# Small projection as 392 columns of one product, and a local values product on half the columns

## The reference

```python
qa, ka, va, ga, qi, ki, wi, qb, kb, vb, gb = jnp.split(proj, offsets, axis=-1)
# group A, blocks of 128 queries: an indexer scores the keys, the best 256 are kept
dots = jnp.einsum('bqhd,bsd->bqhs', qi_blk, ki)                   # 4 heads of 64
score = jnp.einsum('bqh,bqhs->bqs', w_blk * idx_scale, jax.nn.relu(dots))
_, idx = lax.top_k(jnp.where(visible[None], score, -jnp.inf), 256)
...                                                   # softmax attention over these, 8 heads
# group B: attention in a window of 128, 8 query heads on 2 key heads, a sink per head
out = jnp.einsum('bckgqs,bcskd->bcqkgd', p, v_band)
...
y = jnp.concatenate([ya * silu(ga), yb * silu(gb)], axis=-1) @ w_out
x = layer_norm(ALPHA * x + y, ln_g, ln_b)
```

## Time and profile before

| | |
|---|---|
| median of 3 runs | 1456.59 us (1453.73 to 1456.72) |
| the profiled execution | 1462.23 us, of which its span is 1460.4 us |
| TensorE (PE) busy | 1359.3 us, 93% |
| VectorE (DVE) busy | 1130.6 us, 77% |
| ScalarE (ACT) busy | 896.8 us, 61% |
| GpSimd (POOL) busy | 629.6 us, 43% |
| mean granted TensorE clock | 0.964 |

### The profile page before, as it was taken

One profiled execution on the slowest core, in us unless ns is written; L12 is line 12 of the kernel. 1 busy time (PEld: TensorE's weight loads), 2 busy tenths in 40 slices (PEclk: granted clock), 3 DMA queues, 4 the chain that ended last, 5 costly groups with the idle time before them and its releaser, 6 DMA issues. The chain is left out here.

```text
span 1460.4 us, 18810 instructions
## 1 busy us (share of the span) xinstructions
PE 1359.3 (93%) x6006; PEld 993.5 (68%) x6052; DVE 1130.6 (77%) x2215; ACT 896.8 (61%) x1687; POOL 629.6 (43%) x726
## 2 busy tenths in 40 slices
PE   7999999899999995798999799999999799999997
PEld 5888887698888874565655456655555565588886
DVE  3486879864899887778889999889898967257675
ACT  3395885873498736777775488885678676700010
POOL 2421332633422336466544256534336577423332
PEclk9999999999999996699999999999999899999999
DMA  7412232325232328233433132402011143134442
GB/s 241 127 60 80 87 105 80 117 91 154 73 109 94 101 90 174 66 89 87 113 92 88 45 83 56 104 21 64 27 28 26 39 133 118 44 122 146 144 148 83
DMA packets 106548, 136.85 MB, mean 94 GB/s; under 512 B 6643, under 2 KB 83383, under 8 KB 106191
## 3 DMA queue, kind: packets, MB, share of 16 engines
q1 hardware_dynamic: 93296, 93.23, 23.4%
q10 hardware_dynamic: 9504, 31.66, 5.5%
q0 software_dynamic: 3648, 10.76, 2.5%
HBM read 92.20 MB, written 42.34 MB: 92 GB/s over the span
## 5 line engine op out<-in xcount | busy, mean ns | idle before, releaser
L1644 DVE TENSOR_SCALAR_CACHE_REDUCE above<-dist,trial 128x512 bf16<-128x512 int32 (+13 forms) x224 | 345.9, 1544 | 28.9 <-POOL trial L1002 23.9
L1179 ACT ACTIVATE above<-dist,trial 128x384 bf16<-128x384 int32 (+13 forms) x224 | 280.8, 1254 | 60.8 <-DVE trial L1617 24.3
L1356 PE MATMUL psum<-x_hi,w_hi 128*128 128x512 f32 x640 | 251.8, 393 | 16.0 <-DVE x_lo L1693 10.6
L1356 PE MATMUL psum<-x_lo,w_hi 128*128 128x512 f32 x640 | 250.8, 392 | 0.0
L1356 PE MATMUL psum<-x_hi,w_lo 128*128 128x512 f32 x640 | 250.5, 391 | 0.0
L1290 ACT ACTIVATE prob<-psum 128x512 f32<-128x512 f32 x272 | 159.8, 593 | 115.8 <-PE psum L1506 54.6
L1748 DVE CUSTOM_DVE_ANT_0 junk<-psum,mask 128x512 bf16<-128x512 f32 (+3 forms) x320 | 184.4, 605 | 26.7 <-PE psum L1430 16.1
L1506 PE MATMUL psum<-prob,vw 128*65 128x512 f32 x376 | 184.8, 597 | 0.1
L1493 PE MATMUL psum<-qa_mix,ka_mix 128*128 128x512 f32 x272 | 162.4, 597 | 5.5 <-DMA qa_ext<-minus_max 3.7
L1430 PE MATMUL psum<-ka_ext,qa_ext 128*128 128x512 f32 (+3 forms) x320 | 134.1, 467 | 27.4 <-ACT ka_mix L1129 12.3
L941 POOL CAST w_hi<-raw 128x1024 fp32r<-128x1024 f32 x40 | 49.7, 1243 | 253.1 <-PE psum L1356 248.8
(11 more groups left out here) (161 smaller groups left out, 2906.8 us busy)
## 6 DMA issues: line engine op xcount, KB each, us to landing
raw<-w_tiles SPq DMA_DIRECT2D x40, 512.0 KB, 3.7
proj<-staged ACTq DMA_DIRECT2D x40, 512.0 KB, 3.3
qb_raw<-proj SPq DMA_DIRECT2D x32, 256.0 KB, 4.0
qa_raw<-proj SPq DMA_DIRECT2D x32, 256.0 KB, 4.5
yt_raw<-y_t SPq DMA_DIRECT2D x16, 512.0 KB, 5.1
x_row<-x_res SPq DMA_DIRECT2D x16, 512.0 KB, 3.9
out<-z ACTq DMA_DIRECT2D x16, 512.0 KB, 2.6
x_raw<-xT SPq DMA_DIRECT2D x12, 512.0 KB, 4.2
```

The source lines that it names most:

```text
L1179: nc.scalar.activation(above[:, 0, 0:n], src, ACT.Sign, scale=-1.0, bias=u, accum_out=count[:, 0:1]).then_inc(sign_counted, 1)
L1356: last = pe.matmul(psum[:, 2 * u + m, :], wt[:, u, k, :], xt[:, k, 512 * m:512 * m + 512], start=(k == 0 and q == 0), stop=(k == KT - 1 an ...
L1644: v.tensor_scalar(above[:, 1, 0:n], src, u, None, ALU.is_ge, ALU.add, accum_out=count[:, 1:2]).then_inc(own_counted, 1)
```

## The change

Four things are edited. (1) The two parts of the small weights lie in one tile `wn`, so that the high part of x is multiplied by high and low weights in one matmul of 392 columns; the low part of x then adds its 196 columns to the first half. A block has 16 matmuls in place of 24. (2) The two halves of the result are summed on leaving PSUM: ACT copies the low half into `vw` (`low_norm`), DVE adds the high half (`leave_norm`), and only then is the bank free. (3) `mix_b` multiplies only the 64 value columns of its key head and writes rows 0 to 63 or 64 to 127 of bank 2 alone; `gate_b` becomes one multiplication over 128 rows. (4) Many costs of the plan, the delays in `AFTER` and every number of `PREFER` are different, and with them the order on all engines.

```diff
-AFTER = {..., "store_masks": 3.5, "load_keys_a": 5.0, "keys_rest": 4.0, "extra_rows": 4.0, "shift_values": 4.0}
+AFTER = {..., "store_masks": 4.5, "load_keys_a": 6.0, "keys_rest": 7.0, "extra_rows": 8.0, "shift_values": 14.0}
-PREFER = {'above': -36689.1, 'band0': -163507.6, ...}
+PREFER = {'above': -116549.4, 'band0': -205923.3, ...}
...
-        add("PE", 2.62, "norm", b, ...
+        add("PE", 2.2, "norm", b, ...
-        add("ACT", 0.55, "leave_norm", b, needs=[("norm", b)])
+        add("ACT", 0.55, "low_norm", b, needs=[("norm", b)])
+        add("DVE", 0.6, "leave_norm", b, needs=[("low_norm", b)])
...
-        add("PE", 1.8, "mix_b", b, needs=[("copy_b", b), ("shift_values",)], holds="banks2", until=("gate_b", b))
-        add("DVE", 1.35, "gate_b", b, ...
+        add("PE", 0.95, "mix_b", b, needs=[("copy_b", b), ("shift_values",)], holds="banks2", until=("gate_b", b))
+        add("DVE", 0.71, "gate_b", b, ...
...
-                wn_hi = sb(early, "wn_hi", [P, KT, VN], F32R)
-                wn_lo = sb(early, "wn_lo", [P, KT, VN], F32R)
+                wn = sb(early, "wn", [P, 2, KT, VN], F32R)
...
-            def leave_norm(b):
+            def low_norm(b):
                 i = NORM_ORDER.index(b)
                 act.wait_ge(norm_mm, i + 1)
                 bank = 4 + 2 * (i % 2)
-                copy(vw[:, b, 0:HD], psum[:, bank, 0:HD])
-                copy(vw[:, b, HD + 1:VN + 1], psum[:, bank, HD:VN]).then_inc(norm_out, 1)
+                copy(vw[:, b, 0:HD], psum[:, bank, VN:VN + HD])
+                copy(vw[:, b, HD + 1:VN + 1], psum[:, bank, VN + HD:2 * VN]).then_inc(norm_low, 1)
...
                 for k in range(KT):
-                    for q, (xt, wt) in enumerate(((x_hi, wn_hi), (x_hi, wn_lo), (x_lo, wn_hi))):
-                        last = pe.matmul(psum[:, bank, 0:VN], xt[:, k, toks], wt[:, k, :],
-                                         start=(k == 0 and q == 0), stop=(k == KT - 1 and q == 2))
+                    pe.matmul(psum[:, bank, 0:2 * VN], x_hi[:, k, toks], wn[:, :, k, :], start=(k == 0), stop=False)
+                    last = pe.matmul(psum[:, bank, 0:VN], x_lo[:, k, toks], wn[:, 0, k, :], start=False, stop=(k == KT - 1))
...
                         keys = vw[:, BLOCKS[b], HD + 1:HD + 1 + P] if c else vs[:, BLOCKS[b], :]
-                        last = pe.matmul(psum[:, 2 + g, 2 * P * c:2 * P * c + 2 * P], keys, ptb[:, g, 2 * P * c:2 * P * c + 2 * P],
+                        rows = slice(HD * g, HD * g + HD)
+                        last = pe.matmul(psum[rows, 2, 2 * P * c:2 * P * c + 2 * P], keys[:, rows], ptb[:, g, 2 * P * c:2 * P * c + 2 * P],
                                          start=True, stop=True)
...
+            def leave_norm(b):
+                i = NORM_ORDER.index(b)
+                dve.wait_ge(norm_low, i + 1)
+                bank = 4 + 2 * (i % 2)
+                v.tensor_tensor(vw[:, b, 0:HD], psum[:, bank, 0:HD], vw[:, b, 0:HD], ALU.add)
+                v.tensor_tensor(vw[:, b, HD + 1:VN + 1], psum[:, bank, HD:VN], vw[:, b, HD + 1:VN + 1],
+                                ALU.add).then_inc(norm_out, 1)
...
-                for g in range(2):
-                    rows = slice(HD * g, HD * g + HD)
-                    last = v.tensor_tensor(yt_b[rows, :, :].rearrange("p h (c q) -> p c h q", c=2),
-                                           psum[rows, 2 + g, :].rearrange("p (c h q) -> p c h q", c=2, h=4),
-                                           gate_b[rows, :, :].rearrange("p h (c q) -> p c h q", c=2), ALU.mult)
-                last.then_inc(b_gated, 1)
+                v.tensor_tensor(yt_b[:, :, :].rearrange("p h (c q) -> p c h q", c=2),
+                                psum[:, 2, :].rearrange("p (c h q) -> p c h q", c=2, h=4),
+                                gate_b[:, :, :].rearrange("p h (c q) -> p c h q", c=2), ALU.mult).then_inc(b_gated, 1)
```

More of the change, by code:

```diff
@@ L70 @@
+IN_ORDER = ("round_x", "split_x", "split_x2", "round_w", "split_w", "evacuate", "store", "norm", "low_norm", "leave_norm", "dots", "relu",
             "sum", "exp_b", "exp_a", "logits", "values", "scan", "scan_max", "copy_b", "turn_b", "window", "bias_b", "positions",
@@ L204, in dots_of @@
             add("ACT", 0.12 + 0.84 * w / 512, "relu", *part, needs=[("dots", *part)])
-            add("DVE", 0.25 + 1.05 * w / 512, "sum", *part,
+            add("DVE", 0.15 + (1.57 if h else 1.3) * w / 512, "sum", *part,
                 needs=[("relu", *part), ("leave_norm", BLOCKS[2 * p + j]), sums[-1], ("masks", p - 1)])
@@ L224, in dots_of @@
         add("DVE", 0.25 + n * 0.00116, "equal", p, needs=[("limits", p)])
-        add("DVE", 0.9 + n * 0.0077, "masks", p, needs=[("equal", p), ("above", p)])
+        add("DVE", 0.9 + n * 0.0092, "masks", p, needs=[("equal", p), ("above", p)])
         add("ACT" if p < 5 else "SP", 0.7, "store_masks", p, needs=[("masks", p)])
@@ L274, in norm @@
         i = NORM_ORDER.index(b)
-        add("PE", 2.62, "norm", b, holds=f"banks{4 + 2 * (i % 2)}", until=("leave_norm", b),
+        add("PE", 2.2, "norm", b, holds=f"banks{4 + 2 * (i % 2)}", until=("leave_norm", b),
             needs=[("split_x", KT + 1), last_norm[0]] +
@@ L323, in whole_plan @@
     add("ACT", 0.25, "put_sink", 0, needs=[("setup_dve",)])
-    add("SP", 0.8, "shift_values", needs=[end, ("leave_norm", NORM_ORDER[-1])])
+    add("SP", 3.6, "shift_values", needs=[end, ("leave_norm", NORM_ORDER[-1])])
     stores = [("store", 1, N_TILES - 1), ("store", 1, N_TILES - 2)]
```

50 lines of the change are left out of this document (25 added, 25 removed).

## The result

| | before | changed |
|---|---|---|
| median | 1456.5 us (1453.7 to 1456.7, 4 runs) | 1463.8 us (1462.9 to 1465.7, 4 runs) |
| profiled execution | 1462.2 us | 1463.5 us |
| PE busy | 1359.3 us | 1343.4 us |
| VectorE busy | 1130.6 us | 1126.4 us |

The changed kernel is slower: the ratio is 1.0058, interval 1.0046 to 1.0071. The forecast was 1441, range 1428 to 1459, slower at 0.15: wrong in sign and outside the range. TensorE has 16 us less to do and the span is 1 us longer.

What follows compares the result with a forecast made beforehand. TensorE bounds only stages it fills; VectorE's chain of searches limits the first stage. Terms -4 - 4 - 3.4 - 2 - 2 = -15.4 us take the profiled 1462.2 to 1446.8; forecast median 1441 us, its own range 1434 to 1449, overall 1428 to 1459.

Steps and rivals of the forecast that it cites:

- part 3: Last score sums to first scan: setup and bias pieces fit VectorE's 8.2 us of gaps; first scan -4 us.
- rival 2: Keys land late behind SP's queue, over 12 us from last sum to first rounding; 1459 us, chance 0.14.
- part 2: Norms' new places in the projection stage: 6.6 us gained, 5 lost; with other terms dots 4 move -1.6 us.
- The 5 us of waiting at norms 11 and 8 and at product (1, 3): Projection stage, around search 3: banks freed late by two engines cost 3.5 + 1 + 0.5 us, bounds 0 and 9.
- 11.4: Late stage: gain of the mix_b edit, the gate and crowded place, and the moved band work together, in us.
- Mix_b: Local values product: 1.5 us instead of 1.73, 3.4 us over 15 blocks, bounds 0 to 12.9.
- rival 1: Two halves of mix_b overlap fully, 0.87 us each instead of 1.5: 9.5 us more, 1432 us, chance 0.20.
- Sortable 6: Crowded place, 780 to 860: one wait of up to 9 us replaces several; 2 us gained.
- my step from the profile to the median: Profiled execution of before stands 5.6 us above its median, so 1446.8 us profiled became a forecast of 1441.
- the norm at 2.3 us: Small projection: a block takes 2.30 us instead of 2.66, 0.36 us a block, 5.8 us in all.
- VectorE's gate: gate_b: two half-partition multiplications become one, 0.69 us a block, 11 us of VectorE.
- Rival 3: Late stage bound by searches of VectorE and ScalarE, so 11.4 us of gains vanish into waits; 1453 us, chance 0.16.

Runs made afterwards that it cites:

- a_front: Changed kernel with single pieces moved: last relus and sums, bias and key loads and key roundings earlier, some band work behind the second scan; 1460.2 us, ratio 1.0029.
- a_keys: Changed kernel with the bias load issued earlier and roundings of queries and bias pieces moved by the plan's own lever; 1490.4 us, ratio 1.0236.
- a_sort: Changed kernel with one VectorE piece moved: leave_max 8 ahead of sortable 6 instead of behind it; 1466.7 us, ratio 1.0083.
- b_both: Kernel before with both edits (small projection, local values product with its gate), in the order of before; 1456.6 us, ratio 1.0004.
- b_best: Kernel before with both edits in its old order, but norms 4, 5, 0 and 9 moved with what leaves their banks; 1441.7 us, ratio 0.9901.
- mix_same: 64-column local values product in the order of before, both key heads on array columns 0 to 63; mix_b 1.87 us, one execution 1460.8 us.
- ba: Changed work in the order of the kernel before up to the last score sum of pair 5, then in the changed order; 1469.6 us, ratio 1.0096.

## Why the prediction was wrong

- **The failing step is the way into the late stage (part 3), forecast -4 us at the first scan, measured +20.6.** Of these, 5.3 us stand already at dots 4 (next point), 15.3 arise behind it. I counted VectorE's gaps as room for the setup and the bias pieces, and asked only whether the keys' load would be late behind SP's queue. It was not here (7.2 us, rival 2 decides at 12), though a_front and a_keys come to 11.7 and 11.8 once the last sum is early. Late were the loads of what had been moved ahead of the sums: the bias (10.8 us) and three inputs of roundings (9.1 us). A gap is room only for work whose inputs are there. A number was at hand, which I did not look up: the bias took 11.6 us to land in the kernel before. a_front puts this step right and gets 3.7 us of the median back, so the step is shown to cost, but it is not the whole loss.
- Within that, -1.6 us at dots 4 (part 2) became +5.3 (349.9 to 356.2 in the seven kernels that have this work and order up to there). The 5 us of waiting at norms 11 and 8 and at product (1, 3) were 1.7, all at the product; but norm 2 waits 1.3 for its low weights, dots 3 2.9 instead of 0.8 and the low parts of x 5.2 instead of 4.4. The profile of before could not show these; I had one place in mind and priced no others.
- Behind the first scan the changed kernel gained 19.3 us (684.4 to the output stage, 703.7 before) where I had 11.4. Mix_b was mis-sized: 1.02 us, not 1.5, 10.7 us of TensorE at the full clock for my 3.4. (the earlier trace rows read 1.77, not 1.73; the 1.73 is that of block 3 and others.) There the mechanism of rival 1 was right, which had 0.87. The Trainium skill (TensorE: Matmul & The Clock Gate, Part 3) has both sentences that I weighed; that small products on different column groups run concurrently, the trace bears out. That matmuls start strictly in program order, it does not, and the measurement decides: all four instructions on `vs` start (699.101 to 699.381) before the first on `vw` (699.583), though the program issues the first head's product on `vw` ahead of the second head's on `vs`.
- Sortable 6: forecast 2 us of gain, with a wait of up to 9. The wait is 11.3, and in a_sort, with the piece out of the way, one of 11.9 stands at the next piece that needs VectorE: the place between two steps of block 8 was not to blame.
- The sum on the profiled execution: forecast 1446.8, measured 1463.5, 16.7 off (24.6 at the first scan, 7.9 better behind it). The other 6.1 us are my step from the profile to the median: 5.8 down by the kernel before, and none for the changed one. That step failed too: it took one execution's offset for a constant, where it goes with the granted clock. So most of the loss that the medians show is in no pair of profiles. b_both against the changed kernel shows that it belongs to the order (7.2 us); which of its waits, beyond the 3.7 us of a_front, stays open.
- Right: the norm at 2.3 us, the wait at norm 6 and its slow clock gone, VectorE's gate, the additions hidden. That b_best reaches 1441.7 with both edits in another order is no support: its gain is made of other terms (4.0 the places, 5.8 the norm's edit, of which I let less than 2 arrive, 4.0 mix_b and gate, where I had 5.4). The order, from which I had the rest, gave nothing and cost 7.
- Rival 3 (the late stage does not feel it) holds in part: of 10.7 us of TensorE and 11 us of VectorE, 4 arrive in the old order.

## What to carry to other kernels

Where a change is an edit and a new order together, run the new work in the old order first: here that alone was 7 us faster than the change as it came, and with four moved norms 22. An engine's gap that is filled with moved work must be checked against the DMA of that work, for whatever is queued behind it waits too. And a bank that a second engine has to free is safe only where neither engine has a long piece ahead of it, or where nothing needs the bank until then: a wait moved by a few products (norm 6 to norm 0, sortable 6 to the bias piece) is often the same wait.

## What the runs showed of the hardware

- Plain float32 products on columns 0 to 63 and 64 to 127 run side by side although the program issues the first head's two products, then the second's: single instructions of a pair start 13 ns apart (699.101 and 699.114), pairs 0.215 apart. Eight instructions take 1.02 us, and 1.87 on one half.
- Half the array costs something at its edge: in mix_same the second instruction starts 0.27 us behind the first and the last is followed after 0.31, where 0.215 is the rule, and 1.87 stands against 1.73. The Trainium skill (TensorEngine Tiling, Key Properties) has a drain at a change of tiling mode; if this is it, this trace shows about 0.14 us of it. My row of 64 columns showed none.
- A product of 392 columns and one of 196 by turns take 0.29 us together, the sum of 0.177 (my estimate by columns) and 0.111, though the narrow one is followed after 0.09.
- The same code in the same order reached dots 4 at 349.9 to 356.2 us in seven profiles. A few us in one stage of one profile are no evidence.
- A score sum (SCALAR_TENSOR_TENSOR on VectorE) is slow exactly where a TENSOR_TENSOR of POOL runs beside it. In the profiles before and changed, those of 256 columns with none beside them take 0.48 to 0.49 us, those overlapped for most of their time 2.0 to 2.6; of 512 columns 0.75 and 2.75 to 2.78. So the last sum's 5.02 us instead of 1.62 come from where level_b and split_index of POOL fell.
- The load of the keys (two of 512 KB) took 5.7 to 5.9 us from issue to landing, and 9.6 to 10.4 where it was issued close behind the shift of values and the gates (a_front, a_keys, ba). The bias (256 KB) took 7.2 to 12.8 us, ahead of the shift (11.6 before, 7.3 in a_front) as behind it (9.7 changed).
